# Order of the matmuls in the up products: all on a tile's high weights, then all on its low weights

## The reference, cut to what matters

```python
u = h @ w_in                      # feed-forward: 1024 -> 2 * 2816, split in gate and val
gate, val = jnp.split(u, 2, axis=-1)
gate = depthwise_conv3(gate) + conv_b
f = (gelu(gate) * val) @ w_out    # 2816 -> 1024
# gated blocks: (silu(x @ w_gate) * (x @ w_up)) @ w_down, the same sizes
```

## Time and profile before

| what | value |
|---|---|
| runs | 1253.33 us median of 3 (1253.25 to 1254.57) |
| profiled execution | span 1251.8 us from first to last instruction; no other time of its own is listed |
| TensorE matmul busy | 1221.5 us, 98% |
| weight loads busy | 1052.4 us, 84% |
| VectorE, ScalarE, GpSimd busy | 73%, 54%, 10% |
| mean granted TensorE clock | 0.995 of 2.4 GHz |
| DMA | 214.51 MB, mean 171 GB/s |

### The profile page before, as it was taken

The page is one execution under the profiler, slowest core; times in us unless marked ns, Lnnn a source line. Parts: engine busy times, 40 slices in busy tenths (PEclk is TensorE's granted clock), DMA queues, the critical chain, the costliest instruction groups (busy, mean ns, idle before and its releaser), DMA issues.

```text
span 1251.8 us, 17734 instructions
## 1 busy us (share of the span) xinstructions
PE 1221.5 (98%) x6970; PEld 1052.4 (84%) x6970; DVE 913.0 (73%) x1192; ACT 671.2 (54%) x1058; POOL 126.1 (10%) x256
## 2 busy tenths in 40 slices
PE   7999999999999998999999999999999999999997
PEld 7899888888879987888888888888797888888886
DVE  6757687878866688977788777666775767666665
ACT  6656544344676776444446745444576445434445
POOL 4000310000120011000001100000107420000002
PEclk8999999999999999999999999999999999999999
DMA  8835276665445444555654465665454126555550
GB/s 242 248 132 162 92 227 202 202 201 187 151 152 169 135 164 131 193 179 199 202 202 147 153 212 187 202 202 193 136 176 168 57 86 219 183 178 174 175 199 34
DMA packets 149014, 214.51 MB, mean 171 GB/s; under 512 B 4410, under 2 KB 114428, under 8 KB 148932
## 3 DMA queue, kind: packets, MB, share of 16 engines
q1 hardware_dynamic: 145612, 205.39, 49.5%
q0 software_dynamic: 1632, 4.71, 1.5%
q10 hardware_dynamic: 1688, 3.28, 0.8%
HBM read 212.30 MB, written 1.06 MB: 170 GB/s over the span
## 4 chain that ended last, share of the span: by engine, by line
PE 86%; DVE 6%; ACT 4%; issue 2%; POOL 1%; DMA 0%; POOLq 0%; ACTq 0%; DVEq 0%
PE work L2153 24%; PE work L2155 12%; PE acc L1776 8%; PE acc L1777 8%; PE acc L1778 8%; PE work L1776 5%; PE work L1777 5%; PE work L1778 5%; PE work L1798 2%; PE work L1965 2%; ACT w_hi L677 1%; PE acc L1941 1%; ACT xn L681 1%; DVE hT_both L1187 1%; DVE w_lo L1178 1%
## 5 line engine op out<-in xcount | busy, mean ns | idle before, releaser
L1178 DVE TENSOR_TENSOR w_lo<-raw,w_hi 128x2048 fp32r<-128x2048 f32 x195 | 441.9, 2275 | 29.8 <-ACT w_hi L677 29.8
L2153 PE MATMUL work<-hT_both,w_hi 128*128 128x512 f32 x1280 | 455.1, 398 | 0.0
L677 ACT ACTIVATE w_hi<-raw 128x2048 fp32r<-128x2048 f32 x195 | 368.8, 1896 | 6.0 <-DMA raw<-in_na_w_qkv 6.0
L2155 PE MATMUL work<-hT_both,w_lo 128*128 128x256 f32 x1280 | 359.1, 281 | 0.0
L2153 PEld LDWEIGHTS work<-hT_both,w_hi 128*128 128x128 f32 x1280 | 240.5, 188 | 58.6
L2155 PEld LDWEIGHTS work<-hT_both,w_lo 128*128 128x128 f32 x1280 | 241.6, 189 | 3.0
L1776 PE MATMUL acc<-w_hi,aux_hi 128*128 128x512 f32 x400 | 158.2, 395 | 2.8 <-DVE aux_lo L1530 2.8
L1777 PE MATMUL acc<-w_lo,aux_hi 128*128 128x512 f32 x400 | 156.6, 391 | 0.0
L1778 PE MATMUL acc<-w_hi,aux_lo 128*128 128x512 f32 x400 | 155.8, 390 | 0.0
L1504 DVE TENSOR_REDUCE Z<-work 128x256 f32<-128x512 f32 x88 | 60.5, 688 | 81.6 <-PE work L2155 78.8
L548 POOL TENSOR_SCALAR ms<-ssq 128x1 f32<-128x1 f32 x30 | 16.9, 565 | 902.5 <-ACT Z L681 461.4
(11 more groups left out here) (242 smaller groups left out, 1867.2 us busy)
## 6 DMA issues: line engine op xcount, KB each, us to landing
raw<-in_ffn_w_in SPq DMA_DIRECT2D x44, 1024.0 KB, 6.0
raw<-in_ffn_w_out SPq DMA_DIRECT2D x22, 1024.0 KB, 5.1
raw<-in_w_gate SPq DMA_DIRECT2D x22, 1024.0 KB, 5.5
raw<-in_w_up SPq DMA_DIRECT2D x22, 1024.0 KB, 5.9
raw<-in_w_down SPq DMA_DIRECT2D x22, 1024.0 KB, 5.0
raw<-in_na_w_qkv SPq DMA_DIRECT2D x12, 1024.0 KB, 7.8
raw<-in_da_w_qkv SPq DMA_DIRECT2D x12, 1024.0 KB, 5.4
raw<-in_ple_w_gate SPq DMA_DIRECT2D x8, 1024.0 KB, 5.3
```

The source lines that it names most:

```text
L677: act.activation(w_hi[:, n % RING, 0:size], raw[:, n % RAW, 0:size], ACT.Copy).then_inc(hi_done, 1)
L1178: dve.tensor_tensor(w_lo[:, n % RING, 0:size], raw[:, n % RAW, 0:size], w_hi[:, n % RING, 0:size].bitcast(F32), ALU.subtract).then_inc(lo_ ...
L2153: pe.matmul(b.rearrange("p (e s) -> p e s", e=2), v[0][:, k, cols(c % 2)], hT_both[:, k, :, :], start=k == 0, stop=False)
L2155: ins = pe.matmul(b[:, 0:S], v[1][:, k, cols(c % 2)], hT_hi[:, k, :], start=False, stop=k == KT - 1)
```

## The change

In `up(c)` the loop over the eight blocks of the contraction is split in two. The eight matmuls of 512 columns on the high weights come first, then the eight of 256 columns on the low ones. The count and the shapes of the matmuls, the waits and the semaphores stay.

```diff
                         for k in range(KT):
                             pe.matmul(b.rearrange("p (e s) -> p e s", e=2), v[0][:, k, cols(c % 2)], hT_both[:, k, :, :],
                                       start=k == 0, stop=False)
+                        for k in range(KT):
                             ins = pe.matmul(b[:, 0:S], v[1][:, k, cols(c % 2)], hT_hi[:, k, :],
                                             start=False, stop=k == KT - 1)
                         ins.then_inc(bank_full[(g + i) % WORK], 1)
```

## The result

The kernel after takes 1247.5 us (median of 5 runs, 1246.88 to 1248.6) against 1253.76 (1253.25 to 1255.42): ratio 0.9949, 95% interval 0.9939 to 0.996. That is 6.3 us less, and the interval leaves out 1; the forecast was 6.1 less and 1247.2. The profiled executions differ by 5.9 us of span. I read the page's head first, then the groups of the two lines.

What follows compares the result with a forecast made beforehand. The prediction took TensorE's own matmul pace as the bound; 77 x -0.08 + 3 x 0.04 = -6.1 us off the median of 1253.33 gave 1247.2 us, with a range of 1244.6 to 1250.9.

Steps and rivals of the forecast that it cites:

- The bound: In the steady tiles of all four phases only TensorE's own pace counts: busy 165.41 us of 165.41.
- The sum for one tile: Up tile: long and short runs of 1.81, 0.95, 1.84, 0.95 us, 0.08 less than 5.64; down tile keeps 2.75.
- The tiles behind transposes: Three of the 80 up tiles begin behind transposes and would take 5.67 us instead of 5.63, 0.04 more.
- 77 x -0.08: All up tiles but the three behind transposes gain 0.08 us each, -6.2 us in total.
- The cover of 2.35 us: VectorE finishes `aux_lo` 2.35 us before the down tile needs it, against 0.08 us of gain per tile.
- Carried in full: At phase ends, the next phase starts earlier by the phase's whole gain, 20 x 0.08 = 1.6 us.
- Rival A: Up tiles: the pace belongs to the operands, not the order; tile stays 5.64 us, time 1253.3; chance 12%.
- Rival B: Long run behind a short one does not settle in six; gain 0.06 or 0.01 a tile, 1248.5 to 1252.5; 10%.
- Rival C: Long runs of the new order pay no switch cost; up and down tile 0.13 us less, 1243 us; 5%.
- Rival D: Weight loads exposed in short runs set the pace at 192 ns; +82 us less the 6, 1329 us; 3%.

Runs made afterwards that it cites:

- e1: The kernel after with each bank's matmuls in groups of two long, two short, four times, instead of eight and eight; 1246.99 us, ratio 0.9947 against the kernel before.
- e7: The kernel before (old alternating order) with one transposition of the identity ahead of each up tile; 1260.28 us, ratio 1.0055.
- e2: The kernel after with each bank's matmuls in groups of four long, four short, twice, instead of eight and eight; 1251.03 us, ratio 0.9977 against the kernel before.
- e6: The kernel after with each short matmul of 256 columns cut in two of 128; 1383.03 us, ratio 1.1036 against the kernel before.
- e4: The kernel after with each up tile reordered over both banks: nine long, sixteen short, seven long; 1252.95 us, ratio 0.9994 against the kernel before.
- e8: e4's order from tile 3 on, tile 2 in the order of the kernel after; 1246.4 us, ratio 0.9945 against the kernel before.
- e11: e8 with three idle-time matmuls, results unused, ahead of the transposes that open the mixer; 1245.64 us, ratio 0.9938 against the kernel before.
- e10: The kernel after, unchanged, measured again beside e8; 1247.13 us, ratio 0.9951 against the kernel before.
- e3: The kernel after with sixteen long matmuls over both banks of a tile, then sixteen short; 1254.85 us, ratio 1.0007 against the kernel before.
- e12: e8 unchanged, measured again beside e11; 1246.1 us, ratio 0.9937 against the kernel before.

## Why the prediction was right, step by step

**The bound** was read rightly: TensorE's pace in the four phases, without idle time. All of the change came from start intervals, with counts, durations and the other engines' work as they were.

**The sum for one tile** was right in every term: 1.81, 0.95, 1.84, 0.95 and 2.75 were forecast, 1.81, 0.96, 1.84, 0.95 and 2.75 came. The mixer's runs of six carried over to runs of eight with other operands, because a long run settles after five and a short one after two. That was known only for runs this long: the same reasoning missed e1 by 3.6 us. The total is better than its working deserves. Executions of the kernel after spread over 1.7 us, the interval allows a gain of 5.0 to 7.6 us, and the median of before rose from 1253.33 to 1253.76 with two more runs, so a miss of 0.3 us is in part luck; the 0.01 us of the tile is not.

**The tiles behind transposes** were forecast at 5.67 (now 5.63); in the profile after, such a tile runs from 294.70 to 300.38, 5.68:

```profile
294.70 2.09 PE L2153 MATMUL work<-hT_both,w_hi 128*128 128x512 f32 x8
...
300.38 0.40 PE L1776 MATMUL acc<-w_hi,aux_hi 128*128 128x512 f32 x1
```

**"77 x -0.08"** counted two tiles too many, the first up tile of the two feed-forward phases. The down tile behind it waits for VectorE's `aux_lo` in both kernels. In the first of them after:

```profile
166.33 0.43 DVE L1530 TENSOR_TENSOR aux_lo<-Z,aux_hi 128x256 fp32r<-128x256 f32 x1 [0.48 <-ACT aux_hi L971]
166.90 0.47 PE L1776 MATMUL acc<-w_hi,aux_hi 128*128 128x512 f32 x1
```

`aux_lo` ends at 166.76 and the down tile starts 0.14 later. From the up tile's start to that of the next it is 8.47 us, 161.28 to 169.75; before, it was 161.10 to 169.57, the same 8.47. The tile's 0.08 is lost in that wait. In the second feed-forward phase it is 8.47 after (501.30 to 509.77) and 8.45 before (502.51 to 510.96). The cover of 2.35 us that I had read from a later tile isn't there at the start of such a phase. In the SwiGLU phases, whose VectorE has no convolution, the first tile gained in full:

```profile
720.13 1.98 PE L2153 MATMUL work<-hT_both,w_hi 128*128 128x512 f32 x8
...
725.69 0.40 PE L1776 MATMUL acc<-w_hi,aux_hi 128*128 128x512 f32 x1
```

That is 5.56. So 75 x 0.080 = 6.0, less 0.13 for the three tiles behind transposes and 0.01 in the second feed-forward phase, gives 5.86 us, which is also what all 80 up and down tiles sum to (671.06 before, 665.20 after). The spans differ by 5.90.

**"Carried in full"** held. From the first tile of each of the four phases to that of the next (for the fourth, to the end) the time fell by 1.39, 1.38, 1.82 and 1.49 us; the tiles of each had given 1.40, 1.39, 1.60 and 1.48. The 0.22 beyond that in the third holds the mixer, where both profiled executions had the clock low once. The 0.18 by which the first tile starts later after (161.10 and 161.28), with the same kernel ahead of it, takes most of it back.

**Rival A** (the pace belongs to the operands) is dead: the first bank's eight long ones, with stationary weights and `hT_both` moving, take 1.81. The formula of the Trainium skill (TensorE: Matmul & The Clock Gate, Back-to-back issue gap), in which order plays no part, would have given no change. The page offers it for isolated matmuls, and this is a stream with weight loads; 0.080 us a tile and the two paces of e7 speak against using it for one. **Rival B** (no settling) did not appear: the second bank's run took the 1.84 of a settling one and the down tile 2.75. Such runs exist, though: e2's down tile takes 2.77, and behind e6's matmuls of 128 columns it takes 2.82. **Rival C** (no entry cost) neither. **Rival D** (exposed loads) had a real floor near it: e6 shows 112 ns, and with 8 ns between it and 120 the short run stayed clear. Its 192 ns, the listed duration of a load, was never the pace.

## What to carry to other kernels

On an engine that never waits, read the cost of a matmul from start to start, by run length and by what stands ahead, and look for another stretch of the same trace that already has the order you want; here it gave the tile to 0.01 us. A theory made from such rows is safe only for run lengths that they hold: mine failed for runs of two. Grouping matmuls by length pays only a few nanoseconds per pair, and less than an early request for a slab can cost: e4's tiles were better by 0.02 us each and the kernel slower by 5.5. The best version that ran at a measurable distance from before, e8 (e11 with the filled wait), is 7 to 8 us under the kernel before. Under the one after it is 0.7 beside it (e8 against e10) and at most 1.9 (e11 against 1247.5), at the edge of what these measurements tell apart.

## What the runs showed of the hardware that I had not expected

- The cost of mixing lengths isn't steady in the run length: 8.386, 8.293, 8.353, 8.307 and 8.287 us per up and down tile for runs of one, two, four, eight and sixteen (the last in e3, 170.93 to 286.95 over 14 tiles). Runs of two beat runs of four and eight. What holds this lag in the engine is open; no view shows it.
- The same instructions run at two paces, 5.64 and 5.73 us a tile in e7; a tile keeps the pace that it begins with, and what sets it is open.
- A matmul of 128 columns with its own weight load costs 112 ns in a run, hardly less than one of 256 at 120.
- The granted clock fell to its lower level in some executions and not in others, behind waits that all of them have: 2.4 us at the mixer (e8, but not e10) and 1.8 us in the second feed-forward phase (e11, but not e12). The stretch around it took 0.8 us more in e8 and 1.6 in e11, of a total of some 1246.
